# Hybrid encoder layer on one core: small loads moved behind the first weights, one-hot slot products held back until the output projection has ended

## The reference

```python
def token_mixer(a, ...):
    p = a @ w_in                       # 1024 -> 1216: q latent 384 | kv latent 256 | rope key 64 | pool 512
    c_q, c_kv, k_r, u = jnp.split(p, [384, 640, 704], axis=-1)
    q = (rms_norm(c_q) @ w_uq)         # 4 heads of 192
    kv = (rms_norm(c_kv) @ w_ukv)      # 4 heads of 128 + 128
    # per-head rms norm of q and k, rotary part of 64, full attention
    attn = bidirectional_attention(q, k, v)
    pool = multi_scale_pool(u, w_pool, pool_scale)
    return jnp.concatenate([attn, pool], axis=-1) @ w_out

h = x + token_mixer(rms_norm(x), ...)
# 4 groups of 8 experts: best group by softmax, then the best two experts in it
for e in range(32):
    hdn = jax.nn.silu(a @ w_gate[e]) * (a @ w_up[e])
    y = y + combine[:, e:e + 1] * (hdn @ w_down[e])
x = h + y
```

## Time and profile before

| | |
|---|---|
| three runs | 649.23, 649.58, 647.74 us |
| the profiled execution | 643.12 us, of it 641.5 us span |
| granted TensorE clock, mean | 0.955 |
| PE busy | 537.6 us (84%) |
| DVE / ACT / POOL busy | 216.9 / 168.7 / 137.8 us |
| DMA | 140.69 MB, mean 219 GB/s |
| chain that ended last | DMA 44%, PE 42%, DVE 6% |

### The profile page before, as it was taken

How to read it: one execution, slowest core, us unless ns; L and a number is a source line. 1 busy time by engine, 2 the same in 40 slices (tenths; PEclk the granted TensorE clock), 3 DMA queues, 4 the chain that set the end, 5 groups by cost and what they waited for, 6 DMA issues and landing times.

```text
span 641.5 us, 9145 instructions
## 1 busy us (share of the span) xinstructions
PE 537.6 (84%) x3140; PEld 380.6 (59%) x3141; DVE 216.9 (34%) x646; ACT 168.7 (26%) x412; POOL 137.8 (21%) x214
## 2 busy tenths in 40 slices
PE   3979999999898889899962989999878995778861
PEld 2859888887344477788852546665546653444540
DVE  2663342351768662445573111121111111111110
ACT  3563434332464521222331201121111111111100
POOL 6022321321154100011114002321201321101110
PEclk9989999999899999999985989999999999988887
DMA  8920000000432009433359979999999999999961
GB/s 202 379 104 22 13 34 1 0 1 1 170 100 65 1 33 372 180 130 112 100 188 370 351 230 393 382 370 379 381 368 415 393 382 360 375 379 389 395 233 20
DMA packets 28589, 140.69 MB, mean 219 GB/s; under 512 B 6339, under 2 KB 7078, under 8 KB 16246
## 3 DMA queue, kind: packets, MB, share of 16 engines
q1 hardware_dynamic: 20496, 122.89, 49.1%
q0 software_dynamic: 6288, 14.04, 9.2%
q10 hardware_dynamic: 1766, 3.25, 1.7%
HBM read 131.15 MB, written 16.46 MB: 230 GB/s over the span
## 4 chain that ended last, share of the span: by engine, by line
DMA 44%; PE 42%; DVE 6%; SPq 2%; issue 2%; ACT 2%; POOL 1%; POOLq 0%
DMA expert_w<-in_w_down 20%; DMA expert_w<-in_w_up 18%; PE ps L450 8%; PE ps L451 7%; PE ps L455 7%; DMA w_uq_raw<-in_w_uq 3%; PE ps L615 3%; PE ps L556 3%; PE ps L779 2%; PE ps L570 2%; DMA x_res<-in_x_prompt 2%; DMA g_rows<-token_rows,idx_all 1%; PE ps L795 1%; PE ps L573 1%; SPq L369 1%
## 5 line engine op out<-in xcount | busy, mean ns | idle before, releaser
L779 PE MATMUL ps<-expert_w,xT 128*64 128x256 f32 x1152 | 131.2, 384 | 19.7 <-DMA expert_w<-in_w_up 8.3
L779 PEld LDWEIGHTS ps<-expert_w,xT 128*64 128x64 f32 x1152 | 96.8, 138 | 58.0 <-issue 29.4
L795 PE MATMUL ps<-expert_w,hT 128*64 128x512 f32 x288 | 73.9, 659 | 18.7 <-DMA expert_w<-in_w_down 13.2
L1544 POOL DMA_INDIRECT out<-y_sb,idx_now x18 | 28.7, 1596 | 190.2 <-issue 142.2
L1387 DVE SCALAR_TENSOR_TENSOR hid<-s_act,gate,ps 128x256 f32<-128x256 f32 x18 | 12.0, 667 | 144.4 <-ACT s_act L1025 144.4
L795 PEld LDWEIGHTS ps<-expert_w,hT 128*64 128x64 f32 x288 | 24.9, 150 | 56.1 <-issue 56.1
L1025 ACT ACTIVATE s_act<-ps,gate 128x256 f32<-128x256 f32 x18 | 8.5, 473 | 134.3 <-PE ps L779 134.3
L450 PE MATMUL ps<-w_in_hi,aT_hi 128*128 128x384 f32 (+2 forms) x120 | 43.7, 369 | 0.0
L1399 DVE COPY y_sb<-ps 128x512 f32<-128x512 f32 x18 | 12.4, 692 | 86.3 <-PE ps L795 86.3
L451 PE MATMUL ps<-w_in_lo,aT_hi 128*128 128x384 f32 (+2 forms) x120 | 40.9, 345 | 0.0
L1030 ACT ACTIVATE y_sb<-ps 128x512 f32<-128x512 f32 x18 | 10.7, 597 | 89.6 <-PE ps L795 89.6
(11 more groups left out here) (235 smaller groups left out, 927.7 us busy)
## 6 DMA issues: line engine op xcount, KB each, us to landing
expert_w<-in_w_gate SPq DMA_DIRECT2D x32, 1024.0 KB, 9.5
expert_w<-in_w_up SPq DMA_DIRECT2D x32, 1024.0 KB, 9.1
expert_w<-in_w_down SPq DMA_DIRECT2D x32, 1024.0 KB, 9.8
w_in_raw<-in_w_in SPq DMA_DIRECT2D x8, 608.0 KB, 19.3
w_out_raw<-in_w_out SPq DMA_DIRECT2D x8, 512.0 KB, 3.8
out<-h_sb SPq DMA_DIRECT2D x6, 512.0 KB, 4.6
token_rows<-h_sb ACTq DMA_DIRECT2D x6, 512.0 KB, 4.9
x_sb<-in_x_prompt SPq DMA_DIRECT2D x4, 512.0 KB, 10.5
```

The source lines that it names most:

```text
L779: mm = pe.matmul(ps[r, 2, g * FH:(g + 1) * FH], xT[:, q.o, k, r], w_gu(b, lane, k, g), start=(k == 0), stop=(k == KD - 1))
L795: mm = pe.matmul(ps[r, 4 + half, :], hT[:, q.o, k, r], w_dn(b, lane, k, half), start=(k == 0), stop=(k == 1))
L1544: pool.indirect_dma_start(out=out, out_offset=bass.IndirectOffsetOnAxis(ap=idx, axis=0), in_=y_sb[:, buf, :], in_offset=None, compute_op=A ...
```

## The change

It does two things.

1. The 14 small loads leave POOL's queue for SP's. The seven that the rotary table needs stand behind `w_ukv`, ahead of the third x tile. The other seven (`small_tables`) are issued right behind the fourth x tile, and the fold of `g_router` into `w_router` moves from tile 1 to tile 4 on DVE.
2. `slot_a` and `slot_b` get five buffers (`SLOT_BUFS`). PE's products for tile 0 stand at the last tile of the projection loop; `slots` of tiles 1 to 4 stand behind the last logits and ahead of the last ranks; `more_slots` of tiles 1 to 5 stand at the very end. The waits for a free buffer become waits for the tile five before.

```diff
@@ SP
+            def small_tables():
...
+                        sp.dma_start(dst, src).then_inc(router_in, 16)
...
+                sp.dma_start(out[T:T + P, :], a["zeros"]).then_inc(setup_dram, 16)
...
             sp.dma_start(w_ukv[:, :, :], a["w_ukv"][0].rearrange("(k p) n -> p k n", k=KKV)).then_inc(w_ukv_in, 16)
+            small = [(rope_tab[:, :, :, :].rearrange("p n t r -> p (n t r)"), a["rope"])]
...
+                for dst, src in small:
+                    sp.dma_start(dst, src).then_inc(gains_in, 16)
...
             for i in range(2, NT):
                 sp.wait_ge(x_sq, i - 1)
                 sp.wait_ge(x_tr, 2 * (i - 1))
                 load_x(i)
+                if i == 3:
+                    small_tables()
@@ PE
-                if i >= 2:
-                    slots(i - 2)
-                    more_slots(i - 2)
+                if i == NT - 1:
+                    slots(0)
+                    more_slots(0)
...
             logits(NT - 1, 1)
-            slots(NT - 2)
-            more_slots(NT - 2)
+            for i in range(1, NT - 1):
+                slots(i)
             ranks(NT - 1)
             slots(NT - 1)
...
-            more_slots(NT - 1)
+            for i in range(1, NT):
+                more_slots(i)
@@ ACT and DVE
-                if i >= 1:
-                    act.wait_ge(slot_mm, i)
-                    act.wait_ge(more_mm, i)
+                if i >= SLOT_BUFS:
+                    act.wait_ge(slot_mm, i - SLOT_BUFS + 1)
+                    act.wait_ge(more_mm, i - SLOT_BUFS + 1)
@@ DVE
-                if i == 1:
+                if i == 4:
                     dve.wait_ge(router_in, 16 * N_ROUTER)
@@ POOL
-                for dst, src in small:
-                    pool.dma_start(dst, src).then_inc(gains_in, 16)
...
-                    pool.dma_start(dst, src).then_inc(router_in, 16)
...
-            pool.dma_start(out[T:T + P, :], a["zeros"]).then_inc(setup_dram, 16)
             step(pool.memset(neg_half[:, :], -0.5))
```

More of the change, by code:

```diff
@@ L47 @@
 NO_TOKEN = 1024
+SLOT_BUFS = NT - 1
 C_ID, C_LTRI, C_IOTA = 0, P, 2 * P
@@ L364, in load_x @@
                 sp.dma_start(x_sb[:, i % 2, :], x_dram(i)).then_inc(x_in[i % 2], 16)
+            def small_tables():
+                with nc.allow_non_contiguous_dma(reason="short rows"):
+                    for dst, src in ((tok_ids[:, :], a["tokens"]),
+                                     (w_router[:, :, 0:EG], a["w_group_router"][0].rearrange("(k p) n -> p k n", k=KD)),
+                                     (w_router[:, :, EG:], a["w_expert_router"][0].rearrange("(k p) n -> p k n", k=KD)),
+                                     (g_router[:, :], a["g_ffn_norm"][0].rearrange("(k p) -> p k", k=KD)),
+                                     (g_x[:, :], a["g_ffn_norm"][0].rearrange("(p k) -> p k", k=KD))):
+                        sp.dma_start(dst, src).then_inc(router_in, 16)
+                sp.dma_start(slot_table.rearrange("(a b) c -> a (b c)", a=P),
+                               a["slots"].rearrange("(a b) c -> a (b c)", a=P)).then_inc(setup_dram, 16)
+                sp.dma_start(out[T:T + P, :], a["zeros"]).then_inc(setup_dram, 16)
             load_x(0)
@@ L372, in _ @@
             sp.dma_start(w_ukv[:, :, :], a["w_ukv"][0].rearrange("(k p) n -> p k n", k=KKV)).then_inc(w_ukv_in, 16)
+            small = [(rope_tab[:, :, :, :].rearrange("p n t r -> p (n t r)"), a["rope"])]
+            half = DR // 2
+            for n, name in enumerate(("g_q_head", "g_k_head")):
+                g = a[name][0:1, DN:DQK]
+                small += [(g_rope[:, 2 * n, :], g.partition_broadcast(P)),
+                          (g_rope[:, 2 * n + 1, 0:half], g[:, half:DR].partition_broadcast(P)),
+                          (g_rope[:, 2 * n + 1, half:DR], g[:, 0:half].partition_broadcast(P))]
+            with nc.allow_non_contiguous_dma(reason="a few hundred short rows"):
+                for dst, src in small:
+                    sp.dma_start(dst, src).then_inc(gains_in, 16)
+            assert len(small) == N_GAINS
             for i in range(2, NT):
```

38 lines of the change are left out of this document (11 added, 27 removed).

## The result

The changed kernel took 630.25, 631.96, 632.55 and 633.5 us, a median of 632.25 us; four runs of the kernel before on the same chip have a median of 649.14 us. The ratio is 0.9741 (95% interval 0.9711 to 0.9770), a gain of 16.9 us. The profiled execution took 630.25 us (span 628.6), the one before 643.12 us.

The account below looks back on a forecast made before the run. It took a rigid stretch of expert loads behind a line of dependent work as the bound; 9.6 us (start) plus 2.7 (projection) made 12.3, taken from the 649.2 us median: 636.9 us, range 633.5 to 642.0.

Parts of the forecast that it names:

- PE's clock behind `c_transposes`: Products of `w_uq` behind `c_transposes` may find PE fast instead of slow: up to 1 us, outside the sum.
- the median of the runs is 6.1 us above it, and the change is taken from that: Whole kernel: gain read from the 643.12 us profile is subtracted from the 649.2 us median.
- Start, up to `c_transposes`: Start of the kernel: with the small loads moved, `w_uq` lands at 21.8 us, `c_transposes` start at 26.8: 9.6 us gained.
- The count of slow blocks: PE on the `w_in` blocks at the start: one slow (3.3 us), one mixed (2.0 us), six fast (9.9 us).
- open point: PE's pace at the start: granted clock reads 1.00, yet three matmuls take 1.38 us in one block, 0.72 in another.
- Projection: Projection loop: slot products leave PE in three tiles net, 0.89 us each, 2.7 us gained.
- Behind the projection: After the projection: moved `slots` (2.0 us) and longer `more_slots` (3.7 us more) are hidden by waits and cost nothing.
- B: Rival, tail not covered: late `more_slots` delay pair 0 and expert loads by up to 3.7 us; 640.6 us, chance 0.04.
- The rotary loads: Start, SP's queue behind `w_ukv`: six broadcasts overlap and land at 28.7 us, before DVE needs them, at no cost.
- D: Rival: rotary broadcasts land one after another, p us each, DVE waits; gain gone at p = 3.3, slower beyond; chance 0.05.
- A: Rival: start gains only 6.8 to 7.9 us, from a 325 GB/s queue or one more slow PE block; 639.7 us, chance 0.15.
- C: Rival: short rows don't fill the DMA engines, `w_uq` still lands near 32 us; 643.9 us, chance 0.06.

Follow-up runs that it names:

- slots_only: Kernel before with only the slot products held back and five slot buffers, small loads still on POOL's queue at the start: 644.75 us, ratio 0.9946.
- rope_late: Kernel before with only the seven rotary loads moved to SP's queue behind `w_ukv`, and the `g_router` fold at tile 4: 640.79 us, ratio 0.9906.
- router_late: Kernel before with only the five router loads and two fills moved to SP behind the fourth x tile, `g_router` fold at tile 4: 644.05 us, ratio 0.9943.

## Why the prediction was right and where it fell short

**Which steps failed.** The forecast gain was 12.3 us, the measured one 16.9. Two steps failed. First, the sum has nothing for PE's clock behind `c_transposes`, which the bounds name and put at up to 1 us; it measured 2.1 us in the means. Second, "the median of the runs is 6.1 us above it, and the change is taken from that" holds the distance between the profiled execution and the median constant. It was 6.0 us before and is 2.0 after. Between the first two profiles the change is 12.9 us, close to 12.3, and in part by luck: 1.5 us each from the clock and the end of the program stand against 2.4 us that this pair lost in attention. The other 4.0 us of the 16.9 come in by the second step. The clock alone would have moved the forecast to 634.8 us, still inside the range. By the means of the profiles the small terms all but cancel (start -0.2, projection +0.1, end +1.4, attention -1.2, gather to last scatter-add -0.1), the clock adds 2.1, and 2.4 us are in no profile.

**What bounds the kernel: right.** A rigid stretch of expert loads (245.9 us for 244.7 in the chain) behind a line of dependent work. What was taken off ahead of it came off the end.

**Start, up to `c_transposes`: right, with a wrong reason inside.** Predicted 21.8 us for `w_uq` and 26.8 for `c_transposes`, measured 22.3 and 26.35: a gain of 10.0 us in the first pair of profiles and 9.4 in the means, for 9.6. The rates hold (373 to 420 GB/s), so the rate of the rows was the right one to use. It was not the 358 GB/s that the Trainium skill gives in "DMA: Bandwidth & Descriptors" (section Specifications), and the measurement decides. The count of slow blocks holds as well. Timeline after, first three matmuls of blocks 0, 1 and 2, for the earlier trace rows:

```profile
9.86 1.35 PE L501 MATMUL ps<-w_in_hi,aT_hi 128*128 128x384 f32 x3 [2.51 <-ACT w_in_hi L889]
...
13.03 0.89 PE L501 MATMUL ps<-w_in_hi,aT_hi 128*128 128x384 f32 x3
...
14.86 0.73 PE L501 MATMUL ps<-w_in_hi,aT_hi 128*128 128x384 f32 x3
```

One slow, one mixed, then fast, with the starts 3.2 and 1.8 us apart, as assumed. The "open point" there, a granted clock of 1.00 beside slow matmuls, has a plain answer: the trace before has no clock record ahead of 24.5 us, the one after none ahead of 13.4, and a window without a record prints 1.00. The paces are the better witness in that stretch. What was wrong is the account of all 14 loads as one body of short rows, "most of their rows between 4 and 256 bytes", and with it "Engines that are full at a third of the rate are moving short rows". The packets that hold the engines are POOL's of 1 and 2 KB, about 1 us each; the six broadcasts do more than all the 4-byte rows, and the table costs little. Since the change moves them all, the sum did not suffer.

**Clock behind `c_transposes`: the mis-sized term.** "the products of `w_uq` behind it may find PE fast, where it was slow after its wait; I put that at up to 1 us" stood in the bounds only, with nothing in the sum. It measured 1.5 us in the first pair of profiles and 2.1 in the means (2.5 to 2.7 where the profile before had the long form). The whole start thus gave 11.5 us, past the stated bound of 11. The bound was derived from one slow block and not from the stretch itself: the granted clock of 38 to 42 us was there to be read.

**Projection: right.** 3 x 0.89 = 2.7 us predicted; 2.8 measured, 2.7 in slots_only. The 3.2 us that stands for it in the forecast's lower end has no working, and no run shows it.

**Behind the projection: right.** Timeline after, for the earlier trace rows:

```profile
318.16 2.00 PE L745 MATMUL ps<-slot_b,slot_a 128*128 128x96 f32 x16
...
322.64 0.19 PE L737 MATMUL ps<-m_sum,bf_consts 128*128 128x32 bf16 x1 [2.48 <-DVE m_sum L1295]
...
327.52 4.55 PE L755 MATMUL ps<-slot_b,slot_a 128*128 128x96 f32 x20 [0.92 <-DVE idx_all L1382]
...
335.33 1.02 POOL L1532 DMA_INDIRECT more_rows<-token_rows,idx_now  x1 [0.96 <-POOL idx_now L1573]
...
337.31 1.97 PE L795 MATMUL ps<-consts_sb,g_rows 128*128 128x128 f32 x8 [5.24 <-DMA g_rows<-token_rows,idx_all]
```

`slots` of four tiles take 2.0 us, as predicted, and PE still waits 2.5 us for the ranks. `more_slots` take 4.55 us, predicted 4.7 (1.0 and 3.7). PE is free 5.2 us before the first gathered rows land. The second gather is issued at 335.3 us, 9.1 us earlier than before, and nothing waits for it: B fell.

**The rotary loads: half wrong, at no cost.** They were to land at 28.7 us, laid over each other. They land one after another, as D supposed, at 25.6, 26.3, 27.6, 29.3, 31.4 and 33.7 us. DVE's fold in the timeline after, for the earlier trace rows:

```profile
33.69 1.43 DVE L1151 TENSOR_TENSOR rope_tab<-rope_tab,q_x 128x256 f32<-128x256 f32 x4 [2.97 <-DMA q_x<-in_g_k_head]
...
35.16 0.95 DVE L1165 TENSOR_REDUCE stats<-junk 128x4 f32<-128x768 f32 x1
```

DVE waits 2.97 us for the last broadcast. By the prediction's own formula, 25.8 + 6p, its landing at 33.7 us is p = 1.3 us: neither laid over each other (p near 0.5) nor the 3.3 us at which D begins to eat the gain. The slack took most of it, for the reduction behind it comes at 35.16 us, 9.0 us earlier than before and 1 us later than the rest of the gain asks for. The next tile and all behind it come 11.5 us earlier (its `c_transposes` at 48.98 us for 60.49). D fell, but its mechanism is the one row of the profile after where the change costs something.

**Rivals A and C** fell with the rows at 420 GB/s and the landing at 22.3 us.

**What the sum did not have at all.** The end of the program, 1.4 us shorter in the means, was taken as rigid; 1.1 us of it are POOL's `DRAIN`. Attention, 1.2 us longer in the mean, was taken to move along unchanged. The two nearly cancel, which is luck.

**What stays open.** The profiles tell of 14.5 us, the timed runs of 16.9. The cause of the difference is open. The five profiles of the kernel before average 645.7 us, and its timed medians 646.4 to 649.3; for the kernel after it is 631.3 and 631.4 to 632.3. In which stage a usual execution of the kernel before spends the 2.4 us more isn't shown by any profile.

## What to carry to other kernels

Broadcasts of one short row on GpSimd's queue belong behind the first weights (whether another queue alone would do is untested); look for a window in which the DMA share is 1 and the rate is a third, and then at the packets of each queue. Before a difference is taken from the median, ask whether the distance between profile and median is part of what the change touches; a second profile shows it. When a wait of some microseconds is removed ahead of TensorE, add what the clock gives back, read from the granted clock of the microseconds behind the wait and not from the window that holds it. And where GpSimd works on float32 in SBUF beside VectorE, cut its instructions short: four pieces instead of one gave 2.4 to 5.5 us here, for some 4 us more of GpSimd's own time (32 pieces of 0.73 us for 8 of 2.37), which nothing waited for.

## What the runs showed of the hardware that I had not expected

- Six broadcast loads that write 128 KB delay `w_uq` by 4.7 us on POOL's queue, a table of 512 KB beside them by nothing (by 2.1 us without them), and the router's seven loads, with 512 KB of zeros among them, by 2.8. On POOL's queue the six are 96 packets of about 1 us each, on SP's 768 packets of 0.011 to 0.018 us. Even there they are slow to land: the window of 25 to 30 us holds little but them, and moves 39 GB/s, now at a share of 0.16.
- The granted clock need not fall within PE's gap. In the ten profiles with a gap of 1.4 us or more ahead of `c_transposes` it falls between 0.6 us before the gap's end (rope_late) and 2.7 us after it (router_late). In the five profiles of the kernel before it then stays at 1.2 GHz for 3.4 us (two) or 6.8 us (three), which are the 6.6 and the 7.7 to 7.8 us to `w_ukv`. The price in the ten was 1.5 to 2.7 us on top of the gap.
- POOL's closing `DRAIN` takes 0.08 us for each transfer that POOL has issued in the whole program, 5.22 us for 63 and 4.08 for 49, though the 14 early ones were done 600 us ago. In this program nothing hides it: it is the last thing that runs.
- A single VectorE multiplication of 0.49 us can take 2.6 us for the sake of one GpSimd subtraction, and a shift of the stage by 1.1 us, between two executions of one program, was enough to change what VectorE lost from 7.1 to 4.4 us.
